# Delta-rule heads: keys and queries stay unnormalised, their lengths enter as columns, and the first head's opening is put in another order

## What is computed

```
def l2norm(t):
    return t * lax.rsqrt(jnp.sum(t * t, axis=-1, keepdims=True) + NORM_EPS)

q = l2norm(q) * (DN_DK ** -0.5);  k = l2norm(k)          # after conv and silu
kb = kc * bc[..., None]                                  # bc = sigmoid(b)
m = jnp.einsum('nbhid,nbhjd->nbhij', kb, kc) * decay     # strictly lower part, plus identity
rhs = jnp.concatenate([vc * bc[..., None], kb * jnp.exp(G)[..., None]], axis=-1)
sol = lax.linalg.triangular_solve(m, rhs, ...)           # u, w
qk = jnp.einsum('nbhid,nbhjd->nbhij', qc, kc) * decay
# over the chunks:
v_new = u_i - w_i @ state
o = (q * exp(G)) @ state + qk @ v_new
state = state * g_last + (k * exp(G_last - G))^T @ v_new
# at the end:
o = o * lax.rsqrt(jnp.mean(o * o, axis=-1, keepdims=True) + NORM_EPS) * norm_w * silu(z)
```

## Time and profile before

| | us |
|---|---|
| median of 3 runs | 3099.35 |
| lowest, highest | 3098.04, 3099.75 |
| the profiled execution, its own time | 3102.16 |
| its span | 3100.3 |
| busy: PE / POOL / DVE / ACT | 3025.0 / 1752.4 / 1495.9 / 717.2 |

### The profile page before, as it was taken

One profiled execution on the slowest core, in us unless ns is written; L12 is line 12 of the kernel. 1 busy time (PEld: TensorE's weight loads), 2 busy tenths in 40 slices (PEclk: granted clock), 3 DMA queues, 4 the chain that ended last, 5 costly groups with the idle time before them and its releaser, 6 DMA issues.

```text
span 3100.3 us, 41585 instructions
## 1 busy us (share of the span) xinstructions
PE 3025.0 (98%) x15344; PEld 2533.3 (82%) x15344; DVE 1495.9 (48%) x2284; ACT 717.2 (23%) x1445; POOL 1752.4 (57%) x992
## 2 busy tenths in 40 slices
PE   8999999999999999999999999999999999999998
PEld 7888886777888978888888888767778888788887
DVE  3332379666537235332243323786665471453313
ACT  1110124422222423110121102244222133231102
POOL 7666663543456745666656665635343558466664
PEclk9999999999999999999999999999999999999999
DMA  4222321211122312222222233212111224122231
GB/s 157 95 101 101 107 93 44 75 62 55 57 94 92 127 67 88 95 96 101 101 90 95 96 107 107 88 43 74 62 55 62 95 82 143 55 95 95 95 102 69
DMA packets 81089, 272.58 MB, mean 88 GB/s; under 512 B 8416, under 2 KB 16864, under 8 KB 80960
## 3 DMA queue, kind: packets, MB, share of 16 engines
q1 hardware_dynamic: 75808, 264.27, 24.6%
q10 hardware_dynamic: 5024, 5.92, 0.6%
q0 software_dynamic: 128, 0.56, 0.0%
HBM read 268.62 MB, written 2.10 MB: 87 GB/s over the span
## 4 chain that ended last, share of the span: by engine, by line
PE 91%; DVE 6%; issue 1%; ACT 1%; DMA 0%; SPq 0%; ACTq 0%; DVEq 0%
PE acc L652 81%; PE aux L652 8%; DVE dc L1940 1%; PE aux L907 0%; DVE lc L1940 0%; DVE xf L2049 0%; DVE xf L1857 0%; PE aux L1146 0%; DVE dc L2083 0%; DVE xl L1773 0%; DVE xf L1854 0%; DVE ml L1773 0%; DMA xf<-in_xT 0%; DVE gt L2045 0%; PE aux L1291 0%
## 5 line engine op out<-in xcount | busy, mean ns | idle before, releaser
L616 POOL TENSOR_TENSOR wl<-raw,wh 128x1024 fp32r<-128x1024 f32 x496 | 1216.7, 2454 | 80.9 <-ACT wh L1363 40.8
L619 POOL TENSOR_SCALAR wh<-raw 128x1024 fp32r<-128x1024 f32 x480 | 528.5, 1101 | 1232.2 <-PE acc L652 845.7
L652 PE MATMUL acc<-xh,wh 128*128 128x512 f32 (+1 forms) x2688 | 1028.4, 387 | 17.2 <-ACT xh L1363 14.5
L652 PE MATMUL acc<-xh,wl 128*128 128x512 f32 (+1 forms) x2688 | 990.5, 373 | 0.0
L652 PE MATMUL acc<-xl,wh 128*128 128x512 f32 (+1 forms) x2688 | 951.4, 373 | 0.0
L652 PEld LDWEIGHTS acc<-xh,wh 128*128 128x128 f32 x2688 | 516.2, 192 | 108.9 <-issue 22.7
L652 PEld LDWEIGHTS acc<-xh,wl 128*128 128x128 f32 x2688 | 516.6, 192 | 82.7 <-issue 5.7
L652 PEld LDWEIGHTS acc<-xl,wh 128*128 128x128 f32 x2688 | 489.5, 191 | 88.3
L1773 DVE TENSOR_TENSOR hl<-tmp,hh 128x512 f32 x88 | 237.9, 2704 | 81.6 <-ACT hh L1363 81.6
L652 PE MATMUL acc<-hh,wl 128*128 128x512 f32 (+1 forms) x704 | 264.6, 376 | 0.0
L652 PE MATMUL acc<-hl,wh 128*128 128x512 f32 (+1 forms) x704 | 264.6, 376 | 0.0
(11 more groups left out here) (300 smaller groups left out, 4022.7 us busy)
## 6 DMA issues: line engine op xcount, KB each, us to landing
raw<-in_stream SPq DMA_DIRECT2D x496, 512.0 KB, 3.2
xf<-in_xT SPq DMA_DIRECT2D x2, 1024.0 KB, 10.1
bias_back<-in_table ACTq DMA_DIRECT2D x2, 1024.0 KB, 8.3
mraw<-in_memT ACTq DMA_DIRECT2D x2, 1024.0 KB, 5.3
out_xT<-xf SPq DMA_DIRECT2D x16, 128.0 KB, 1.7
gate_w<-in_gate_w ACTq DMA_DIRECT2D x2, 512.0 KB, 5.3
sc<-in_ba_w ACTq DMA_DIRECT2D x2, 256.0 KB, 5.6
mask_bits<-in_masks POOLq DMA_DIRECT2D x1, 416.0 KB, 6.9
```

The costliest lines, as they stand in the source:

```text
L616: pool.tensor_tensor(wl[:, s, :], raw[:, s, :], wh[:, s, :].bitcast(F32), ALU.subtract).then_inc(unit_split, 1)
L619: pool.tensor_scalar(wh[:, s, :], raw[:, s, :], 1.0, 0.0, ALU.mult, ALU.add).then_inc(hi_step, 1)
L652: return pe.matmul(out, w, x, start=start, stop=stop, skip_group_check=True)
```

## The change

Keys and queries are no longer multiplied by their rates. Instead:

- the rows of the system `m` are scaled by `k_rate` = beta / (sum of squares + eps), a column, in place of beta; `vn` takes the same column;
- `vk`, the turned values, is scaled by the length of the key (`v_scale`, a root taken by ACT) and moves from ACT to DVE;
- the query's length and its factor 128^-0.5 enter the output's norm: `o_arg` adds the query's sum of squares times `Q_EPS` to the mean square of the output, and the root and reciprocal of that (`std`, `rate`) scale the output as before.

`k_spread`, `q_spread`, `k_normed` and `q_normed` are gone. New are, on DVE, `k_sum`, `q_sum`, `k_inv`, `k_rate`, `o_arg` (128x4 each) and `vk`; on ACT `v_scale`. In the opening `kk` now comes ahead of the norm columns, the fill parts are 4, 4, 6, 2 and 4 (before `kk`, `norm_cols`, `k_turned`, `m_turned`, `v_turned`) where they were 10, 4, 2, 2 and 2 (before `norm_cols`, `k_spread`, `q_spread`, `kk`, `k_turned`), and DVE does the system of head 0 before the convolution of its values.

The core of the diff:

```diff
-FILL_AHEAD = {(0, "norm_cols"): 10, (0, "k_spread"): 4, (0, "q_spread"): 2, (0, "kk"): 2, (0, "k_turned"): 2,
+FILL_AHEAD = {(0, "kk"): 4, (0, "norm_cols"): 4, (0, "k_turned"): 6, (0, "m_turned"): 2, (0, "v_turned"): 4,
...
# DVE
-            4: [(n - 1, "rate")] + only(n, "decay") + (only(0, "conv2") if n == 0 else []),
-            5: (only(0, "k_normed") if n == 0 else []) + only(n, "silu2") + (only(1, "conv1") if n == 0 else []) + only(p, "z_gate"),
-            6: only(p, "o_normed", "y") + only(n, "q_normed")}.get(s, [])
+            4: only(p, "o_arg") + only(n, "k_sum", "q_sum", "k_inv", "k_rate") + only(p, "rate") + only(n, "decay"),
+            5: (only(n, "silu2") if n else []) + only(p, "z_gate"),
+            6: only(p, "o_normed", "y")}.get(s, [])
...
-    steps = only(h, "t0", "y1", "c1") + (only(h + 1, "conv1") if h else []) + only(h, "qk", "x1", "q_dec") + only(h + 1, "conv0")
+    steps = only(h, "t0", "y1", "c1", "vk") + (only(h + 1, "conv1") if h else []) + only(h, "qk", "x1", "q_dec") + only(h + 1, "conv0")
...
# PE
                     if s == 4:
                         if n < HN:
-                            filled(n, "norm_cols")
+                            if n:
+                                filled(n, "norm_cols")
                             act(n, "exp_g")
                             dve(n, "decay_min")
...
+                        if n == 0:
+                            filled(0, "kk")
+                            dve(0, "silu1")
+                            keys_by_keys(0)
                         if n < HN:
+                            if n == 0:
+                                filled(n, "norm_cols")
                             act(n, "sq1")
                             columns(0, y_sum[:, :])
...
-                    if s == 5 and n < HN:
-                        dve(n - 1, "rate")
-                        spread(n, 0, "k_spread")
-                    if s == 6 and n < HN:
-                        if p >= 0:
-                            dve(p, "o_normed")
-                        else:
-                            dve(n, "k_normed")
-                        spread(n, 1, "q_spread")
...
# ACT
+                def value_scale(n):
+                    drain(l, filled_before(n, "norm_cols"))
+                    dve(n, "k_sum")
+                    done(fn(v_scale2[n % 2][:, :], k_sum[:, :], ACT.Sqrt, scale=0.25, bias=eps_0[:, :]), n, "v_scale")
+
+                def out_root(p):
+                    drain(l, filled_before(p, "rms_cols"))
+                    dve(p, "o_arg")
+                    done(fn(o_rate[:, :], o_rate[:, :], ACT.Sqrt, bias=eps_q[:, :]), p, "std")
...
# DVE
+                def out_arg(p):
+                    pe_(p, "rms_cols")
+                    done(stt_(o_rate[:, :], q_sum3[p % 3][:, :], Q_EPS, B5[:, 2 * CH:3 * CH], ALU.mult, ALU.add), p, "o_arg")
+
+                def key_rate(n):
+                    pe_(n, "norm_cols")
+                    done(ts_(k_sum[:, :], B5[:, 0:CH], 4 * NORM_EPS, None, ALU.add), n, "k_sum")
+                    done(dve.tensor_copy(q_sum3[n % 3][:, :], B5[:, CH:2 * CH]), n, "q_sum")
+                    own(n, "k_sum")
+                    done(dve.reciprocal(k_rate2[n % 2][:, :], k_sum[:, :]), n, "k_inv")
...
+                    act_(h, "v_scale")
+                    pe_(h, "v_turned")
+                    scale = v_scale2[h % 2].rearrange("p (c a) -> p c a", a=1).broadcast_to([P, CH, P])
+                    done(tt_(vk[:, :, :], tiles(B6), scale, ALU.mult), h, "vk")
```

## The result

The changed kernel took 3109.70 us (median of 10 runs, 3105.56 to 3113.82) beside 3099.89 us for the kernel before (median of 10, 3096.54 to 3101.60). The ratio is 1.0031, with a 95% interval of 1.0022 to 1.0039: 9.8 us slower. The forecast was 3103.0, within a range of 3089 to 3110; the measured time lies 0.3 us inside the upper end. The profiled execution of the changed kernel spans 3112.0 us and took 3113.82, the slowest of its ten; that of the kernel before spanned 3100.3. The traces thus lie 11.7 us apart.

A forecast was written before the change was run, and what follows sets the result against it. TensorE, 91% of the chain, bounds the kernel. Per layer: opening +8.0, head 0 -0.9, heads 1 and 2 -6.0, head 3 +0.7, making +1.8; +3.6 in all on 3099.35 gives 3103.0 us, range 3089 to 3110.

The forecast's parts named there:

- The opening: First head of each layer, up to its first product: new order brings that product 8.0 us later per layer.
- its slow clock: Behind the opening's first wait, TensorE's clock falls once to half, costing 1.9 us.
- The stall: TensorE's wait right behind the first `decay_rows`, for `exp_g` and `decay_min`: 5.75 us, up to 7.35.
- Head 0: Level 6 of the first head: `q_spread` goes, -0.9 us per layer; level 5 taken as 0.
- head 3: Level 5 of the last head: `q5` waits for a later root, +0.7 us per layer; no gain at level 6.
- the way from level 5 to the last transposition of heads 1 and 2: `q_spread`, its 3.27 us wait and slow clock go: -3.9 us per head, level 5's +0.7 included.
- all the places of the new waits: TensorE waits behind `decay_rows`, before the opening's first product, before `q5`, the last transposition and heads 1 and 2's first product.
- The wait ahead of `q5`: Level 5 of heads 1 to 3: TensorE waits about 1.4 us for ScalarE's copy.
- Start of heads 1 and 2: `vk` on VectorE in front of the convolution delays `x1`: +0.9 us per head, between 0 and +1.5.
- rival 2: Clock falls more often, at the opening's second waits and ahead of `q5`: 3107 to 3114 us; chance 0.28 with other delays.
- The rule that the prediction used: VectorE instructions with two SBUF inputs and GpSimd's SBUF-reading ones exclude each other; those with at most one go free.

The follow-up runs named there:

- the last kernel: Old opening and three edits to the heads, plus one more part of fill at three places where TensorE waits for n1 or n3: 3080.94 us, ratio 0.9938.

## Why the prediction came out as it did

**What held.** The opening: its slow clock (1.9), `m_turned` at 630.1 (630.08 in the trace) and +8.0 up to the first product (+7.6). The stall was 5.12 us where I had 5.75 (the rows named for it add up to 5.67), but the stage began 0.5 later, so the clock times agree by luck as well. Two parts were right by themselves: `yb_l` took 1.47 us once no split lay on it (3.50 with one, in the kernel with its fill ahead), and the taps of the convolution ahead of `t0` took 5.07. That VectorE's chain from `m_turned` to `x1` took the 16.4 us forecast is luck in part: the other convolution's taps ran clear in 2.32 instead of 5.12, while its scaling took 2.61 instead of 0.5 and the mask `c0` 1.25 instead of 0.42. Against the kernel before, layer 1 shows 5.8, since there that kernel had its own slow stretch, near 2155 us. Head 0 (-0.9, measured -1.1), head 3 (+0.7, measured +0.6 and +0.7), and the way from level 5 to the last transposition of heads 1 and 2 (-3.9, measured -4.1 at all four places) held as well. So did all the places of the new waits. The wait ahead of `q5` is 1.2 us, not 1.4.

**The time** is inside the range by 0.3 us, and that owes something to luck. I had given 0.53 to a result within 6.2 us of no change and 0.30 to a slower one; it was 9.8 us, slower, against +3.6 forecast.

**The step that failed** is *Start of heads 1 and 2*, one of the smallest terms of the sum: +0.9 per head. Its size was off, since `x1` came 1.3 us later, the upper part of its own bound of 1.5. The steps up to the scaling come 1.5 us later and the taps give 0.8 back (4.32 instead of 5.12), but the scaling itself, under a split's first part, takes 0.55 more than the 0.48 it takes alone:

```profile
702.18 1.03 DVE L1955 TENSOR_SCALAR dc<-dx,par 128x512 f32<-128x512 f32 x1
...
701.89 1.05 POOL L629 TENSOR_SCALAR wh<-raw 128x1024 fp32r<-128x1024 f32 x1 [4.47 <-issue]
```

The rest is larger: the wait became 1.82 us, the clock fell behind it at three of four places, and that cost 2.6, 1.5, 3.0 and 0 us. Per layer the term came to +6.7 and +5.6 instead of +1.8. I took the clock into the sum at one wait only, and asked in rival 2 "whether some 2 us suffice" at the opening's second waits and at `q5`, but not here. Rival 2's mechanism and its 3107 to 3114 were right and its places wrong. Behind `q5` (1.2 us) the clock never fell in any trace, and in the opening behind `v_turned` not in this execution. The kernel with `vk` behind `x1` confirms it: 10.5 us, of which 4.3 are waits.

**The split of gains and losses.** I had 12 us given back by the heads and 16 taken by the openings. By the table the openings took 13.4 and the heads gave back 4.7, so the first part was near and the second was not: the 7.1 us of slow clock behind `x1` ate most of what the heads had to give. The kernel with the old opening, with the same heads, is 14 us below the kernel before; its trace has 11.0 us of gain in the heads, with only 2.0 us of slow clock at the four places, and 7.7 in the openings, from profiled executions that lie 21 us apart. So the heads can bring about what I had, where the clock stays up. I had weighed the change's two parts in one sum and did not ask what the one would bring without the other. That is where the useful number lay.

## What to carry to other kernels

A step of 0.7 us moved to another engine is priced by what waits behind it there, and a wait that grows from 0.5 to 1.8 us may cost its length again or more in clock (0 to 3.0 us here): count the waits that a change makes longer, not only those that it makes. A wait should stand behind the independent work that can cover it, never ahead of it. And where fill draws on a queue of prefetched weights, its amount sets the time at which another engine prepares the next ones; adding "free" fill can move that work onto the instructions that the critical engine waits for, so look for it in the new trace.

## What the hardware showed

**The clock and the waits.** In the two stages of all 13 kernels I took every wait of TensorE from 0.9 us on, and the mean granted clock of the 3 us behind it. Behind 128 waits of 0.9 to 1.78 us it was 1.00 without exception. Behind those of 1.81 to 1.84 us for `x1` it lay below 0.97 in 18 of 24, and behind two of 1.81 at another place, ahead of the output's product in the last kernel, in one; behind 2.4 to 2.5 us in 3 of 3; behind 2.84 and 2.85 us ahead of the values' transposition in 6 of 14 only; behind 3.1 to 3.3 in 6 of 6, and behind 5.1 in 12 of 12. So the length is not all of it. What else decides isn't settled here.

**Who is held by a split.** The rule that the prediction used held: under a split's first part `vk` takes 0.68 us, as it does alone, and `k_sum` 0.15 under its second; both read PSUM. The mask `c2` with two inputs in SBUF went from 0.42 to 2.56, and even `k_rate` on 128x4 took 1.62 and 1.54 instead of 0.17. The scaling of a convolution has a single tensor as its input, and I had counted it as free. In the changed kernel (start, us), under a split, which is the second line, and alone:

```profile
631.74 2.61 DVE L1955 TENSOR_SCALAR dc<-dx,par 128x512 f32<-128x512 f32 x1
631.63 2.44 POOL L626 TENSOR_TENSOR wl<-raw,wh 128x1024 fp32r<-128x1024 f32 x1
...
638.26 0.48 DVE L1955 TENSOR_SCALAR dc<-dx,par 128x512 f32<-128x512 f32 x1
```

The Trainium skill's page on SBUF ("SBUF — State Buffer", section "Who interferes with whom") exempts a VectorE instruction with at most one SBUF input only outside the modes that use two ports, and lists `tensor_scalar` among those that can enter them. These rows agree with the full rule; the prediction gave only half of it, and where it says that an instruction with at most one SBUF input goes free, that exception belongs beside it.
